# Expert gate and up matrices in four pieces instead of two, in a decoder kernel with 64 routed experts on one core

## What is computed

```python
def swiglu(x, w_gate, w_up, w_down):
    return (jax.nn.silu(x @ w_gate) * (x @ w_up)) @ w_down

def routed_moe(h, w_router, router_bias, w_gate, w_up, w_down):
    ...
    idx, gates = route(ht, w_router, router_bias)
    ...
    def expert_block(acc, xs):
        e, tok, g = xs
        y = swiglu(ht[tok], w_gate[e], w_up[e], w_down[e])
        return acc.at[tok].add(g[:, None] * y.astype(jnp.float32)), None
```

## Time and profile before

| what | value |
|---|---|
| median of 3 runs | 1503.97 us (1497.26 to 1506.04) |
| profiled execution, its own time | 1502.87 us |
| its span | 1501.0 us |
| PE busy | 1315.6 us, 88% of the span |
| DVE, ACT, POOL busy | 481.3, 250.2, 180.1 us |
| read from HBM | 496.11 MB, 331 GB/s over the span |
| share of the 16 DMA engines, SP's queue | 86.8% |
| mean granted TensorE clock | 0.948 |

### The profile page before, as it was taken

The page is one execution under the profiler, slowest core; times in us unless marked ns, Lnnn a source line. Parts: engine busy times, 40 slices in busy tenths (PEclk is TensorE's granted clock), DMA queues, the critical chain, the costliest instruction groups (busy, mean ns, idle before and its releaser), DMA issues.

```text
span 1501.0 us, 24624 instructions
## 1 busy us (share of the span) xinstructions
PE 1315.6 (88%) x6693; PEld 649.7 (43%) x6694; DVE 481.3 (32%) x1095; ACT 250.2 (17%) x495; POOL 180.1 (12%) x586
## 2 busy tenths in 40 slices
PE   4799799999999999887689978999999999979674
PEld 1374554444444444433236455444444444434231
DVE  1534623222322233212553372322222223213125
ACT  1232211111111111111123221111111111111011
POOL 0001111111111111110000111111111112101010
PEclk9999799999999999988899979999999999989887
DMA  9976549999999999999898664285999999999992
GB/s 352 391 316 236 227 145 375 380 386 355 395 357 381 368 366 393 409 393 409 301 390 316 237 240 147 106 331 202 373 369 382 369 382 366 401 397 410 408 409 92
DMA packets 129959, 497.70 MB, mean 332 GB/s; under 512 B 15081, under 2 KB 15089, under 8 KB 123265
## 3 DMA queue, kind: packets, MB, share of 16 engines
q1 hardware_dynamic: 129920, 497.24, 86.8%
HBM read 496.11 MB, written 1.08 MB: 331 GB/s over the span
## 4 chain that ended last, share of the span: by engine, by line
PE 64%; SPq 10%; DVE 9%; DMA 8%; issue 6%; ACT 2%; DVEq 0%; ACTq 0%
PE ps L814 25%; PE ps L830 12%; PE ps L851 6%; DMA ring<-in_w_exp_up 5%; SPq L412 5%; PE ps L699 4%; PE ps L761 3%; PE ps L771 3%; DMA ring<-in_w_ada 3%; SPq L416 2%; DVE temp L1129 2%; DVE w L1346 2%; PE ps L823 1%; ACT w L978 1%; PE ps L725 1%
## 5 line engine op out<-in xcount | busy, mean ns | idle before, releaser
L814 PE MATMUL ps<-ring,w 128*64 128x512 f32 (+1 forms) x2432 | 438.4, 615 | 78.6 <-DMA ring<-in_w_exp_up 49.7
L814 PEld LDWEIGHTS ps<-ring,w 128*64 128x64 f32 (+1 forms) x2432 | 149.8, 128 | 338.5 <-issue 338.3
L830 PE MATMUL ps<-ring,w 128*32 128x512 f32 (+1 forms) x1216 | 219.0, 597 | 0.0
L1346 DVE SCALAR_TENSOR_TENSOR w<-ps,w 128x256 f32<-128x256 f32 x60 | 29.0, 484 | 479.3 <-ACT w L978 479.3
L761 PE MATMUL ps<-hx,scat 128*128 128x512 f32 x496 | 147.5, 420 | 0.0
L1334 DVE CAST scat<-ps 128x512 fp32r<-128x512 f32 x120 | 83.0, 692 | 167.3 <-PE ps L830 167.3
L851 PE MATMUL ps<-scat 128*128 128x512 f32 x480 | 125.4, 403 | 0.0
L1037 POOL CAST idg<-G 128x4 fp32r (+1 forms) x256 | 40.3, 189 | 689.6 <-PE ps L777 654.9
L978 ACT ACTIVATE w<-ps 128x256 f32<-128x256 f32 x60 | 23.1, 385 | 579.6 <-PE ps L814 579.6
L761 PEld LDWEIGHTS ps<-hx,scat 128*128 128x128 f32 x496 | 84.2, 189 | 61.2 <-issue 50.1
L830 PEld LDWEIGHTS ps<-ring,w 128*32 128x32 f32 (+1 forms) x1216 | 61.6, 125 | 108.6 <-issue 104.1
(11 more groups left out here) (218 smaller groups left out, 929.5 us busy)
## 6 DMA issues: line engine op xcount, KB each, us to landing
ring<-in_w_exp_gate SPq DMA_DIRECT2D x256, 512.0 KB, 8.4
ring<-in_w_exp_up SPq DMA_DIRECT2D x256, 512.0 KB, 9.7
ring<-in_w_exp_down SPq DMA_DIRECT2D x128, 1024.0 KB, 11.0
ring<-in_w_ada SPq DMA_DIRECT2D x48, 1024.0 KB, 8.1
w<-in_w_out SPq DMA_DIRECT2D x2, 4096.0 KB, 23.0
w<-in_w_in SPq DMA_DIRECT2D x2, 2400.0 KB, 19.3
rows<-mod_rows SPq DMA_DIRECT2D x8, 512.0 KB, 4.0
w<-in_w_uq SPq DMA_DIRECT2D x2, 1728.0 KB, 11.7
```

Source lines behind the costliest of these rows:

```text
L814: last = mm(ps[unit * g:unit * g + unit, B_F, :].rearrange("p (q f) -> p q f", q=2), hTb[:, kt, unit * g:unit * g + unit], gate_up(k)[:, : ...
L830: last = mm(ps[unit * g:unit * g + unit, bank, :], midT[:, f, unit * g:unit * g + unit], down_w(k)[:, f, half * 512:(half + 1) * 512], sta ...
L1346: v.scalar_tensor_tensor(mid, ps[:, B_F, F:2 * F], gslot, sil, ALU.mult, ALU.mult).then_inc(s["mid_ready"], 1)
```

## The change

The halves become pieces: `PIECES = 4`, and a piece is two steps kt instead of four. A DMA for gate or up carries 256 KB, 2 KB for each partition. There is one landed semaphore for each piece and slot pair. PE waits for its piece in front of steps 2, 4 and 6 (before: step 4 alone) and for piece 0 ahead of the round. `gu_piece_done` takes the place of `gu_half_done` and is increased three times in a block, after steps 1, 3 and 5; `gu_done` still marks the end. SP waits for each of the four releases in turn and issues four DMAs of 256 KB after each. Every initial load is split in the same way. The down matrices are untouched.

```diff
+PIECES = 4
...
-        gu_landed = [[sem(f"gu_landed{half}_{i}") for i in range(RING // 2)] for half in range(2)]
+        gu_landed = [[sem(f"gu_landed{piece}_{i}") for i in range(RING // 2)] for piece in range(PIECES)]
...
-            def load_gate_up(l, half, slots, experts):
+            def load_gate_up(l, piece, slots, experts):
-                kts = slice(half * KT // 2, (half + 1) * KT // 2)
+                kts = slice(piece * KT // PIECES, (piece + 1) * KT // PIECES)
...
-                        sp.dma_start(dst(slot)[:, kts, :], src[:, kts, :]).then_inc(gu_landed[half][slot // 2], 16)
+                        sp.dma_start(dst(slot)[:, kts, :], src[:, kts, :]).then_inc(gu_landed[piece][slot // 2], 16)
...
-                for half in range(2):
-                    load_gate_up(l, half, (0, 1), (0, 1))
+                for piece in range(PIECES):
+                    load_gate_up(l, piece, (0, 1), (0, 1))
...
-                    sp.wait_ge(s["gu_half_done"], used)
-                    passed(sp)
-                    load_gate_up(l, 0, slots, experts)
+                    for piece in range(PIECES - 1):
+                        sp.wait_ge(s["gu_piece_done"], used * (PIECES - 1) + piece)
+                        passed(sp)
+                        load_gate_up(l, piece, slots, experts)
                     sp.wait_ge(s["gu_done"], used)
                     passed(sp)
-                    load_gate_up(l, 1, slots, experts)
+                    load_gate_up(l, PIECES - 1, slots, experts)
...
+            pe.sem_inc(s["gu_piece_done"], B0 * (PIECES - 1) + PIECES - 2)
...
                             for kt in range(KT):
-                                if kt == KT // 2:
-                                    last.then_inc(s["gu_half_done"], 1)
+                                piece, within = divmod(kt, KT // PIECES)
+                                if kt and within == 0:
+                                    last.then_inc(s["gu_piece_done"], 1)
                                     for q in halves:
-                                        pe.wait_ge(gu_landed[1][q], loads * 64)
+                                        pe.wait_ge(gu_landed[piece][q], loads * 64)
                                     passed(pe)
```

More of the change, by code:

```diff
@@ L335, in decoder_trunk @@
         shsil_ready shmid_ready sel_ready sh_gate_done rank_done table_ready rg_ready
-        sh_landed gu_half_done S_ready gath_done hT_ready gu_done sil_ready mid_ready midT_done midT_ready down_done
+        sh_landed gu_piece_done S_ready gath_done hT_ready gu_done sil_ready mid_ready midT_done midT_ready down_done
         ST_done ST_ready y0_ready y1_ready scat_done sh_free out_done ang_ready hi_ready y_free count_ready key_ready place_ready order_done gc_ready rc_ready pro_link
@@ L476, in _ @@
                 sp.dma_start(down_w(3), lay(w_sh_down, l).rearrange("a (k p) d -> p (a k) d", p=P)).then_inc(s["sh_landed"], 16)
-                for half in range(2):
-                    load_gate_up(l, half, (2,), (2,))
+                for piece in range(PIECES):
+                    load_gate_up(l, piece, (2,), (2,))
                 load_down(l, (2,), (2,))
@@ L485, in _ @@
                 passed(sp)
-                for half in range(2):
-                    load_gate_up(l, half, (3,), (3,))
+                for piece in range(PIECES):
+                    load_gate_up(l, piece, (3,), (3,))
                 sp.wait_ge(s["sh_free"], l + 2)
@@ L525, in _ @@
             tr = nc.tensor.transpose
-            start_counts(pe, "gu_half_done gu_done midT_done ST_done scat_done", "gath_done gT_done down_done",
+            start_counts(pe, "gu_done midT_done ST_done scat_done", "gath_done gT_done down_done",
                          [s["sh_free"], *ada_used])
+            pe.sem_inc(s["gu_piece_done"], B0 * (PIECES - 1) + PIECES - 2)
             pe.wait_ge(s["consts_in"], 16)
```

## The result

| | before | after |
|---|---|---|
| median | 1505.01 us (1497.26 to 1508.05, 4 runs) | 1525.82 us (1517.97 to 1530.58, 4 runs) |
| ratio | | 1.0141, 95% interval 1.0083 to 1.0199 |
| profiled execution, its span | 1502.87, 1501.0 us | 1526.34, 1524.3 us |
| mean granted clock | 0.948 | 0.951 |

The change costs 1.4%, over the 0.5% that a measurement can tell from nothing. The 1505.3 us of the forecast were 20 us short, and the range ended at 1522.

The account below looks back on a forecast made before the run. DMA was taken to bound five one-block cycles, PE the other expert cycles. Terms 8.6 - 1.4 - 0.8 - 5.1 = +1.3 us on a median of 1503.97 gave 1505.3 us, range 1496 to 1522.

Parts of the forecast that it names:

- What bounds: Expert cycles: PE bounds those with four blocks or more; DMA bounds five one-block cycles, each with one long wait.
- The packets, +8.6 us: Full-queue gate and up loads: two 2 KB packets take 7.5 ns more than one of 4 KB, over 1152 packets per engine.
- The lower bound from the router's 425 GB/s: Router-matrix stretch with a few dozen 2 KB packets: taken as their rate, a gain of 3.5%, some 6.5 us.
- In the other cycles the price is covered.: Four-block cycles: loads need 63.4 us, PE 67.0, so 3.6 us are left to hide dearer packets.
- The second rival: Four-block cycles turn DMA-bound because short queues make packets dearer: 14 us, total 1519 us, chance 0.27.
- SP's issue, 0: SP's queue: 16 DMAs take 8.6 us to issue in place of 4.3, but SP keeps ahead, so nothing is added.
- Waits on PE, 0: Gate and up products: two more waits in each block cost nothing when already met.
- Rival three: The added waits on PE cost 0.2 us each in 60 blocks: +24 us, 1529 us, chance 0.05.
- Gaps in the quads, -1.4: Five PE-bound quads that break at half 1: four pieces let DMA start before, saving 1.4 us.
- Dips and last quads, -0.8 and -5.1: DMA-bound quads: earlier start and releases lessen rate dips, -0.8 us; each layer's last quad ends sooner after landing, together -5.1 us.
- The signs that were named: DMA-bound cycles: 396 to 400 GB/s, 1 to 2 us longer, quad waits about 7 us, landing about 10; under 385 wrong.

Follow-up runs that it names:

- e1: Kernel before with 2 KB packets, still 512 KB DMAs and releases and waits in two halves: 1517.09 us, ratio 1.0089.
- e14: Kernel before with 256 KB DMAs of 4 KB packets, each half's four even-partition DMAs first, then the four odd ones: 1499.15 us, ratio 0.9974.
- e9: Kernel before with 256 KB DMAs of 2 KB packets, the two quarters of a matrix issued back to back: 1518.17 us, ratio 1.0103.
- e5: Kernel before with each 512 KB DMA split into even and odd partitions, 256 KB each, 4 KB packets: 1503.69 us, ratio 1.0011.
- e3: The change's 256 KB DMAs with 2 KB packets, a matrix's quarters four DMAs apart, but before's waits and releases in halves: 1565.65 us, ratio 1.0413.
- e4: The change's four waits and four releases, with the 512 KB DMAs of the kernel before: 1502.87 us, ratio 1.0001.
- e12: As e3, but slot by slot, so that the two quarters of a matrix are two DMAs apart: 1549.31 us, ratio 1.0322.
- e10: The change with slots 0 to 3 starting at steps 0, 4, 2 and 6, in loads and products: 1548.18 us, ratio 1.0306.
- e6: The change with three pieces of 4, 2 and 2 steps instead of four equal ones: 1535.32 us, ratio 1.0225.
- e2: Kernel before with each 512 KB DMA split into partitions 0 to 63 and 64 to 127, 4 KB packets: 1911.66 us.

## Why the prediction was wrong, point by point

**What bounds.** Right: five DMA-bound cycles with about 10 us of wait each, the others PE's.

**The packets, +8.6 us.** Right in kind, undersized. Over the whole kernel e1's 38 us of engine time over 4096 pairs of packets on an engine (195,456 packets for 129,920, over 16) is 9.3 ns for a pair, where 7.5 was said. In the full queue, for which the 7.5 was meant, it is more: the DMA-bound stretches of e1 grew by 4.9 us in layer 0 and by 8.5 in layer 1 (176.6 to 185.1), 13.4 us over the 1152 pairs, 11.6 ns each, and e1 as a whole by 1.0089, 13 us. The lower bound from the router's 425 GB/s was no guide. The estimate worked out from the Trainium skill's 3 cycles for a packet (DMA: Bandwidth & Descriptors, Bandwidth), 2.3% for such a pair, is less than half of what was measured: 38 us on the 54% of 1303 us that the routed gate and up matrices are (268 of 497 MB) is 5.4%. The Trainium skill's advice to batch 2 KB transfers into 4 or 8 KB (Perfetto Trace Analysis, DMA Optimizations) speaks against the change, and the runs agree: 4 KB packets turned into 2 KB ones alone cost 0.9% (e1).

**"In the other cycles the price is covered."** This is the step that failed, in two parts. First, the 3.6 us of cover were reckoned at the full queue's rates, 391 and 410 GB/s. The four-block cycles never ran at these: before took 2.63 us per MB in them, not the 2.52 of a DMA-bound cycle, which the earlier trace rows showed (0.97 / 371). With 2 KB packets in e1 it is 2.71; a cycle has 16.8 + 8.4 = 25.2 MB, so 68.3 us of engine time in a cycle of 67.6. The packets were still covered, but with nothing left. Second, the sum had no term for the order of issue. The change issues one quarter of four matrices and then the next quarter of each, and now a megabyte takes 2.80 us, 70.6 us a cycle, and the cycle 70.1 instead of PE's 67. I had read no row on the order, because before reads each matrix in 4 KB runs, and there the order costs nothing (e14).

**The second rival** was what happened: four-block cycles turned DMA-bound, priced at 14 us over two layers, measured 14.6 in layer 0 and 0.4 in layer 1. That its 14 us met 14.6 is partly luck: the 14 was the middle between nothing and 28 over eight cycles. Its mechanism was looked for in a short queue: packets of any size dearer there. That alone doesn't tip the cycles (e1 and e9); it takes the order as well. Its 1519 was 7 us short, mainly since the DMA-bound stretches took 8.7 us more, where the terms for them gave 2.7 (8.6 - 0.8 - 5.1). The argument against it ("a queue that gets behind gets full, and then runs at 410") was wrong: the share was 1.00 to 1.02, and the rate 347 to 374.

**SP's issue, 0.** The number of DMAs costs nothing with 4 KB packets, shown by e5. The time of an issue isn't fixed, though: 0.35 us in the earlier trace rows, 1.0 to 1.3 in e3 under load.

**Waits on PE, 0.** Right: e4 is 1.0001, and a block of L818 with its data is 7.09 us. Rival three falls.

**Gaps in the quads, -1.4.** Wrong in sign: they grew, to 2.62 us in the quad at 312.18, where 0.17 to 0.46 were read before. The piece that PE needs 1.8 us later came later still.

**Dips and last quads, -0.8 and -5.1.** About right in sum. Against e1, which has the packets without the pieces, the change is 1.9 us shorter in layer 0's DMA-bound stretch (117.9 for 119.8) and 2.8 in layer 1's (182.3 for 185.1), 4.7 together where 5.9 were counted (net of what the change's order costs there). In the last quad the final piece is waited for 0.77 us and the products end 1.92 us after it, within the 2 us that were asked for. The dips didn't shrink: the DMA view of the changed kernel from 625 to 645 us still shows one, down to 266 GB/s near 640 us.

```profile
GB/s 406 402 422 422 385 393 422 401 414 426 393 410 414 389 389 389 389 406 393 385 373 389 385 393 385 385 385 361 328 307 275 266 369 373 414 410 418 414 418 410
...
ring<-in_w_exp_gate SPq DMA_DIRECT2D x11, 256.0 KB, 8.8
ring<-in_w_exp_up SPq DMA_DIRECT2D x11, 256.0 KB, 9.4
```

**The signs that were named.** The time to landing in a full queue fell to 9.4 us for the up matrices (rows above), as said ("about 10"). The waits ahead of the quads didn't fall to 7: they are 9.7 to 11.0, since PE starts one piece earlier but on slower bytes; against e1, whose five waits are 63.3 us together, 12.7 each, they did fall, by 2.2 in the mean. The cycle from 599.53 us grew by 1.9 (to 65.16), within the 1 to 2 given, the one from 1357.10 by 3.8 (to 65.50). The rates are 382 to 394 GB/s, below the 396 to 400 given, and 382 and 384 are below the 385 that was to mean wrong.

**What stays open.** Why a 2 KB packet is dearer when the next read of the same 8 KB comes two or four DMAs later. That a change of order alone does it is shown (e9, e12, e3); that it sits in the memory's own organisation would be a guess. Also open is why layer 1's four-block cycles hardly suffered: they took 2.69 to 2.74 us per MB in the change, hardly more than e1's 2.68 to 2.72. Open as well are e10's 1.0306 and e6's idle time.

## What to carry to other kernels

Before a load is cut into more pieces, look at what the cut does to the run of bytes in each partition: the number of DMAs was free here (1.001), 2 KB runs were not (1.009), and 2 KB runs whose row is read again four DMAs later cost more than four times that (1.041). If pieces must be small, issue the pieces of one matrix back to back. And price such a change in the cycles that have little slack, by the engine time per megabyte that those very cycles show (not that of the fullest stretch) against the other engine's time, with the range reaching to where that slack is gone.

## What the hardware showed that was not expected

- The order of the same 256 KB loads with 2 KB runs is worth 3%: 1.0103 back to back, 1.0322 two apart, 1.0413 four apart (e9, e12, e3). With 4 KB runs the order cost nothing (0.9974, e14).
- Loads of 256 KB cut into 64 neighbouring partitions ran at about 240 GB/s, and cut into every second partition at the rate of before: 1911.66 us against 1503.69 for the whole kernel (e2, e5), with SP's queue at 94.0% and 87.0% of the engines.
- A busy DMA engine says little on its rate: at 9 tenths the rate was anywhere from 225 to 434 GB/s within 20 us. The share divided by the rate was the quantity that sorted the kernels.
